# Forty dense V tiles, seven V rows to a group and batches of eight tokens

## The reference, cut to what matters

```python
def peer_ffn(hn, w_pq, sub_keys, u_tab, v_tab):      # 256 tokens, 8 heads, 16 experts a head
    ...
    expert = ia * PEER_N_KEYS + ib                   # ia, ib in 0..127
    gate = jax.nn.softmax(best_s, axis=-1)
    ...
        a = jnp.einsum('td,ted->te', xb, u_tab[eb])  # 128 U rows of 2048 for each token
        hidden = gb.astype(xb.dtype) * jax.nn.gelu(a)
        return jnp.einsum('te,ted->td', hidden, v_tab[eb])   # and 128 V rows
...
h = h + peer_ffn(rmsnorm(h, norm_ffn), ...)
return rmsnorm(h, norm_final)
```

## Time and profile before

| | us |
|---|---|
| median of 3 runs (lowest, highest) | 3092.3 (3092.18, 3098.1) |
| the profiled execution | 3086.04 |
| its span | 3084.2 |
| busy in the span: PE / DVE / ACT / POOL | 2708.9 / 2113.3 / 1146.6 / 976.6 |
| the groups of U rows, from the end of group 0 to the end of group 15 | 868.3 (1876.3 to 2744.6) |
| from there to the first dense product | 81.6 (2744.6 to 2826.2) |
| first to last dense product | 232.2 (2826.2 to 3058.4) |

### The profile page before, as it was taken

How to read it: one execution, slowest core, us unless ns; L and a number is a source line. 1 busy time by engine, 2 the same in 40 slices (tenths; PEclk the granted TensorE clock), 3 DMA queues, 4 the chain that set the end, 5 groups by cost and what they waited for, 6 DMA issues and landing times.

```text
span 3084.2 us, 34635 instructions
## 1 busy us (share of the span) xinstructions
PE 2708.9 (88%) x12198; PEld 1963.7 (64%) x12198; DVE 2113.3 (69%) x2870; ACT 1146.6 (37%) x1980; POOL 976.6 (32%) x566
## 2 busy tenths in 40 slices
PE   8999999999999999999999984666667776679997
PEld 8888788888887888999779881222223332235433
DVE  5687665555564555545555679787888888779877
ACT  5455555555553335445665540000002330034000
POOL 0011000000000000000000027777778877778854
PEclk9999999999999999999999996889898989988999
DMA  6444455555555555543344469999999999999997
GB/s 266 156 155 164 174 178 184 188 190 190 190 178 190 186 184 180 180 178 137 123 178 177 164 240 385 419 415 413 409 417 411 418 412 402 404 399 380 412 410 301
DMA packets 123586, 827.89 MB, mean 268 GB/s; under 512 B 22167, under 2 KB 22183, under 8 KB 23855
## 3 DMA queue, kind: packets, MB, share of 16 engines
q0 software_dynamic: 79392, 510.36, 40.8%
q1 hardware_dynamic: 43920, 313.73, 28.3%
q10 hardware_dynamic: 144, 2.10, 0.2%
HBM read 892.00 MB, written 4.22 MB: 291 GB/s over the span
## 4 chain that ended last, share of the span: by engine, by line
PE 61%; POOL 11%; DMA 11%; DVE 10%; issue 4%; ACT 3%; DVEq 0%; SPq 0%; ACTq 0%
PE ps L608 50%; POOL rows L1310 11%; DMA rows<-peer_u,arena 6%; PE ps L1217 4%; DVE arena L2412 3%; DMA rows<-peer_v 2%; PE ps L1228 2%; DMA rows<-peer_v,arena 1%; PE ps L713 1%; ACT arena L1771 1%; DVE arena L209 1%; DVE arena L202 0%; DVE WL L506 0%; PE ps L908 0%; PE ps L1208 0%
## 5 line engine op out<-in xcount | busy, mean ns | idle before, releaser
L506 DVE SCALAR_TENSOR_TENSOR WL<-ring,PA,WH 128x512 fp32r<-128x512 f32 x896 | 633.4, 753 | 471.0 <-ACT WH L490 454.4
L1228 PE MATMUL ps<-rows,rstd 128*128 128x512 f32 x1164 | 624.4, 689 | 303.9 <-DMA rows<-peer_v,arena 216.8
L2412 DVE CUSTOM_DVE_ANT_0 arena<-rows,arena 128x2048 f32<-128x2048 f32 x256 | 586.9, 2293 | 142.0 <-DMA rows<-peer_u,arena 113.3
L1228 PEld LDWEIGHTS ps<-rows,rstd 128*128 128x128 f32 x1164 | 244.2, 219 | 671.1 <-issue 373.1
L1310 POOL DMA_INDIRECT rows<-peer_v,arena x256 | 473.6, 1850 | 203.8 <-DVE arena L2412 82.6
L489 ACT ACTIVATE WH<-ring,PA 128x512 fp32r<-128x512 f32 x448 | 324.1, 724 | 545.1 <-PE ps L608 398.3
L1310 POOL DMA_INDIRECT rows<-peer_u,arena x256 | 450.9, 1762 | 163.4 <-DVE WL L506 79.8
L608 PE MATMUL ps<-WH,HH 128*128 128x512 f32 x1120 | 442.5, 395 | 4.3 <-DVE WL L506 4.3
L608 PE MATMUL ps<-WH,HL 128*128 128x512 f32 x1120 | 437.6, 391 | 0.0
L608 PE MATMUL ps<-WL,HH 128*128 128x512 f32 x1120 | 437.5, 391 | 0.0
L608 PE MATMUL ps<-HH,WH 128*128 128x256 f32 x1088 | 310.5, 285 | 13.3 <-DVE WL L506 13.3
(11 more groups left out here) (364 smaller groups left out, 3528.5 us busy)
## 6 DMA issues: line engine op xcount, KB each, us to landing
ring<-stream SPq DMA_DIRECT2D x292, 1024.0 KB, 4.8
rows<-peer_v POOLq DMA_DIRECT2D x32, 1024.0 KB, 14.8
rows<-peer_u,arena POOLq DMA_INDIRECT x256, 14.3
rows<-peer_v,arena POOLq DMA_INDIRECT x256, 14.4
arena<-xT SPq DMA_DIRECT2D x4, 512.0 KB, 8.9
bias_rows<-bias_scratch POOLq DMA_DIRECT2D x1, 2048.0 KB, 10.8
arena<-xT ACTq DMA_DIRECT2D x1, 2048.0 KB, 10.1
arena<-memT POOLq DMA_DIRECT2D x1, 2048.0 KB, 9.3
```

The lines of the kernel that those rows point to most:

```text
L506: ins = nc.vector.scalar_tensor_tensor(out=half_tile(WL, u)[:, s], in0=raw_half(u)[:, s], scalar=gain[d], in1=half_tile(WH, u).bitcast(f32 ...
L1228: last = mm(ps[:, 4 * tt + q, :], DIAG[:, k % DIAGS, :], rows[:, SLOTS[n % ROWS], q * CH:(q + 1) * CH], start=n == mine[0], stop=n == ends[q])
L2412: ins = V.tensor_tensor_reduce(out=JUNK, in0=rows[:, SLOTS[n % ROWS], :], in1=HN[:, tt, :], scale=1.0, scalar=0.0, op0=ALU.mult, op1=ALU.a ...
```

## The change

`N_DENSE` goes from 32 to 40, `LEAD` from 9 to 7 and `BATCH` from 16 to 8, which makes 16 batches for a tile of tokens instead of 8, at every fourth U row of groups 9 to 12 and at every second V row of the last part. Fewer lead rows leave more V rows for the last part: 151 instead of 121. Of those that belong to tile 0 (m below 23) DVE now takes every one, so that the sum of tile 0 that PE holds at ROW_LAST is that of the 105 lead rows. The larger matrices need space: IA_GATE and GROW move, the load of GROW now waits for all batches, the last norm writes its result over XN, and the squares of the last norm are written to PSUM.

```diff
-N_DENSE = 32
-LEAD = 9
-BATCH = 16
+N_DENSE = 40
+LEAD = 7
+BATCH = 8
...
     if m < DENSE_FROM:
-        return m % 5 == 4
+        return m % 5 == 4 and N_LEAD + m >= P
...
-    BATCH_AT[ROW_AT["u", 9 + _b // 2, 3 + 8 * (_b % 2)]] = (0, _b)
-    BATCH_AT[ROW_AT["v", *V_ORDER[N_LEAD + 4 * _b + 3]]] = (1, _b)
+    BATCH_AT[ROW_AT["u", 9 + _b // 4, 3 + 4 * (_b % 4)]] = (0, _b)
+    BATCH_AT[ROW_AT["v", *V_ORDER[N_LEAD + 2 * _b + 3]]] = (1, _b)
...
-        GROW = JUNK
+        GROW, _ = take(KD * TOK + KD * P, D)
...
-        FIN = HN
...
-        IA_GATE, _ = take(KD * TOK, 2, BATCH, N_DENSE)
+        IA_GATE, _ = take(N_DENSE * P, 2, BATCH, N_DENSE)
...
-            sp.wait_ge(sem("hidden"), GROUPS)
+            sp.wait_ge(sem("dense_h_kept"), TT * BATCHES)
             sp.dma_start(GROW, bass.AP(gfin_row.tensor, 0, [[0, P], [1, D]])).then_inc(sem("gfin_in"), 16)
             sp.wait_ge(sem("final_ready"), 1)
-            sp.dma_start(out[:, 0, :], FIN[:, 0, :]).then_inc(sem("out_written"), 16)
+            sp.dma_start(out[:, 0, :], XN[:, 0, :]).then_inc(sem("out_written"), 16)
...
-                ch.mark(A(FIN[:, tt, s], XN[:, tt, s], ACT.Square, accum_out=FS[:, n:n + 1]), "final_squares")
+                ch.mark(A(ps[:, 0:4, :].rearrange("p a b -> p (a b)")[:, s], XN[:, tt, s], ACT.Square, accum_out=FS[:, n:n + 1]), "final_squares")
...
-                    V.scalar_tensor_tensor(out=FIN[:, tt, cols], in0=XN[:, tt, cols], scalar=fs, in1=GROW[:, cols],
+                    V.scalar_tensor_tensor(out=XN[:, tt, cols], in0=XN[:, tt, cols], scalar=fs, in1=GROW[:, cols],
...
-                    add_sum(0, 0, 4, done, ROW_DONE[ROW_AT["v", PEER_H - 1, PEER_K - 1]][1])
+                    add_sum(0, 0, 4, done, N_LEAD)
```

More of the change, by code:

```diff
@@ L590, in _ @@
                     sp.dma_start(ring[:, s, :], stream[bass.ds(i * RING + s, 1)].rearrange("a p n -> (a p) n")).then_inc(full[s], 16)
-            sp.wait_ge(sem("hidden"), GROUPS)
+            sp.wait_ge(sem("dense_h_kept"), TT * BATCHES)
             sp.dma_start(GROW, bass.AP(gfin_row.tensor, 0, [[0, P], [1, D]])).then_inc(sem("gfin_in"), 16)
             sp.wait_ge(sem("final_ready"), 1)
-            sp.dma_start(out[:, 0, :], FIN[:, 0, :]).then_inc(sem("out_written"), 16)
+            sp.dma_start(out[:, 0, :], XN[:, 0, :]).then_inc(sem("out_written"), 16)
             for s in range(2):
                 sp.wait_ge(sem("final_ready"), 2 + s)
-                sp.dma_start(out[:, 1, s * HALF:(s + 1) * HALF], FIN[:, 1, s * HALF:(s + 1) * HALF]).then_inc(sem("out_written"), 16)
+                sp.dma_start(out[:, 1, s * HALF:(s + 1) * HALF], XN[:, 1, s * HALF:(s + 1) * HALF]).then_inc(sem("out_written"), 16)
             sp.wait_ge(sem("out_written"), 16 * 3)
```

## The result

The changed kernel takes 3105.7 us in the median of 7 runs (3104.0 to 3109.7), the one before 3091.4 in 7 runs (3085.4 to 3098.1). The ratio is 1.0047, with a 95% interval of 1.0037 to 1.0058: 14.5 us slower, between 11 and 18. The profiled execution took 3107.9 us (span 3106.0).

A forecast was written before the change was run, and what follows sets the result against it. Transfers were taken to bind the groups and dense stretch, DVE the stretch behind ROW_LAST. Terms -69 + 14 + 61 + 2.5 = +8.5 us; 8 us on the 3092.3 median gave 3100 us, range 3084 to 3112.

The forecast's parts named there:

- the forecast's own +6 to +13: Whole kernel: the band of us slower around the summed +8.5 us, given a chance of 0.42.
- DVE binds in the groups too: Rival, chance 0.12: DVE leaves transfers dry 0.5 us more in each group; sum +16.5 us, 3109 us.
- Behind ROW_LAST: From ROW_LAST to the first dense product: DVE sets the pace, 14 us longer, range +13 to +16.
- slots pin the transfers to the same place: At the first dense product POOL can be no further than the twelfth row beyond DVE, cutting whatever the groups gave.
- V rows of DVE under 2.4 us: Sign of being wrong: in the stretch behind ROW_LAST, DVE's V rows take less than 2.4 us.
- Groups: The 15 groups up to ROW_LAST: fewer rows per group, 69 us sooner.
- bound of -64: Smallest gain given for the groups: four groups' 4.4 us DVE excess and a few tenths lost at each choose.
- DVE's need without batches: In a group without batches DVE needs 49 to 50 us of 53.3, a cover of 3 to 4 us.
- Dense stretch: First to last dense product: more dense and V rows, transfers bind, 61 us longer.
- my own upper bound: Dense stretch: 24.6 more full rows at 2.59 us each, 63.7 us longer.
- bytes win: Rival, chance 0.13: transfers stay full behind ROW_LAST, the 17 us saved come through less 2.6 for GROW; about 3078 us.
- GROW: Its 1.05 MB load moves to the first dense product, where bytes bind: +2.5 us.

The follow-up runs named there:

- a_half: Changed kernel, with DVE adding only half the columns of its V rows among the first 35 behind ROW_LAST, same transfers: 3088.3 us, ratio 0.9998.
- b_lead7: Kernel before with LEAD 7 and tile 0's V rows behind ROW_LAST all on DVE; 32 dense tiles and batches of 16 stay: 3104.6 us, ratio 1.0052.
- a_noskip: Changed kernel with no index put out of bounds, so every V row moves all its 128 tokens: 3233.9 us in two runs, ratio 1.0459.
- a_early: Changed kernel with the seven V rows of the last group placed two U rows earlier: 3105.3 us, ratio 1.0043.
- a_dense6: Changed kernel with six products instead of eight for each dense tile, same transfers: 3106.4 us, ratio 1.0048.
- a_dense32: Changed kernel with 32 dense tiles instead of 40; LEAD 7, batches of 8 and the new places stay: 3112.7 us, ratio 1.0066.
- b_place: Kernel before with the new places only: GROW moved and loaded after all batches, last norm over XN, its squares to PSUM: 3090.7 us, ratio 0.9996.
- b_even: Kernel before with always the same 32 of 128 tokens left out of every V row, spread evenly over partitions: 3074.2 us, ratio 0.9945.

## Why the prediction was right or wrong, point by point

The sign, the mechanism and the place were right, and 3105.7 lies in the range; the size was short, 14.5 us for 8.5, and above the forecast's own +6 to +13. Its value is near the rival "DVE binds in the groups too" (3109), but that was not what happened: that rival puts its loss into every group, and of the 72.6 us that the transfers allow, the groups gave 67.4 ahead of the new wait.

**Behind ROW_LAST.** The step that carried the forecast, that slots pin the transfers to the same place and what DVE loses is lost, is shown by a_half and b_lead7, and by a_noskip, where more bytes left that stretch as long as it was. The instruction of 320 columns took 0.49 us, as worked out. The term itself was +11.5 for +14, and the share 0.77 where I had said 0.80. One sign of being wrong was badly put: "V rows of DVE under 2.4 us". The mean of one is 2.35 us in both kernels; the sum used the distance from one to the next, 2.44, and that held (4.82 us for two in the changed kernel).

**Groups.** -62.7 for -69, outside the bound of -64. Two steps failed. I took DVE's need without batches from its waits as 49 to 50 us; groups that run without waits show 50.7, and with four batches 55.0 to 56.2 instead of 54.5. From the end of group 0 to that of group 15 this left -67.4 (864.4 to 797.0 us). The other 4.7 are the wait at the new add. The edit `add_sum(..., N_LEAD)` waits for the last lead row, loaded behind the last U row, where the old one waited for a row seven V rows earlier. I read this line as a mere renaming of a count; a_early leaves open whether it costs anything in the end.

**Dense stretch.** With the groups, this is the term that made the size short: +72.1 in the profiled executions, and at least +65 with the others beside them, for 61 and 2.5. The count of rows was right: 26.1 MB more (120.2 less 94.05) are 24.9 rows, and I had 24.6 and GROW. What was mis-sized is the price of a row: I priced every row by its bytes, at 2.59 us for a full one (405 GB/s). That makes 1.93 us for a V row before and 1.79 after. A full row costs 2.49 us (1.0486 MB at the 421 GB/s of a_noskip). With that for the dense rows, what is left of each dense stretch is the price of a V row: before (232.2 - 29 x 2.49)/80 = 2.00 us, b_lead7 (292.9 - 29 x 2.49)/110 = 2.01, and the changed kernel, with GROW as a 38th full row, (304.3 - 38 x 2.49)/111 = 1.89. So the rate fell to 395 GB/s for two reasons: more of the stretch was V rows, which alone made 400 of 405 (b_lead7), and each had more tokens missing. I took less than my own upper bound because PE would smooth; a_dense6 shows that PE has no part.

**Bytes.** By these prices the 17 us of the "bytes win" rival were not there. Per V row a quarter of tokens missing saved not 0.63 us of 2.49 but 0.45: in the groups, (868.3 - 234 x 2.49)/140 = 2.04 us. With this price 5.7% more tokens left out of 256 rows save 256 x 0.45 x 5.7/25.3 = 26 us, eight dense rows cost 8 x 2.49 = 20, and 6 us are left; 40 tiles against 32 measured about 6 (a_dense32), though with intervals that overlap.

**GROW.** +2.5 expected, nothing found (b_place).

**Two rules that I drew on.** The page "DMA: Bandwidth & Descriptors" of the Trainium skill, section "Why a DMA increments its semaphore by 16 and not by 1", says that a transfer has landed only when all its engines are done. I weighed it for a rival and gave that 0.12. The runs fit it, 418 GB/s with the same tokens left out in every row and 405 as the data falls, but don't show an engine that waits for another. The same page of the Trainium skill, section "Specifications", gives about 358 GB/s as the HBM limit of one core, worked out there as half of what a stack gives two cores. This kernel runs on one core and moved full rows at 421, so the trace doesn't agree with 358 as a limit.

## What to carry to other kernels

Where transfers bind and a ring of slots lies between them and an engine, time is lost in stretches in which that engine is late, and a faster stretch ahead of them can't make up for it by more than the slots hold: count for each stretch what each engine needs, and move no work to the one where another already binds. Bytes saved by leaving out parts of a gather were worth less than their share here (0.45 us for 0.63), except where the same tokens were left out in every row, spread evenly over the partitions. And an edit that turns one count of a wait into another is a new wait: look up what it waits for and when that lands.

## What the runs showed of the hardware that was not expected

The rate of gathers of 128 rows of 8 KB depends on how the tokens left out are spread. The rates are from the rows above. The other two columns are counted from the records that the traces keep of each packet of queue 0 in the dense stretch: a packet of 8192 B is one row of the V table.

| rows in the stretch | left out in a V row | GB/s | mean of an 8192 B packet | over 400 ns |
|---|---|---|---|---|
| all full (a_noskip), 421 in the groups as well | 0 | 421 | 314 ns | 0.05% |
| 80 V and 29 dense rows, same 32 tokens (b_even) | 25.0% | 418 | 315 ns | 0.3% |
| 80 V and 29 dense rows, as the data falls (before) | 25.3% | 405 | 320 ns | 1.4% |
| 110 V and 29 dense rows, as the data falls (b_lead7) | 25.3% | 400 | 321 ns | 1.8% |
| 111 V and 37 dense rows, as the data falls (changed) | 31% | 395 | 325 ns | 2.6% |

The DMA share stands at 0.99 to 1.01 in all of them, so the loss can't be seen in the share, only in the rate. The packets say why the share is blind: a few of them take up to 2.2 us where most take 0.31, and the share counts them as busy. What those over 400 ns take beyond 313 ns each makes 5.4 us of every engine's time in the dense stretch before and 11.6 in the changed one, out of the 8.8 and 18.8 us by which these stretches are longer than their bytes at 421 GB/s. What such a packet waits for is open.

A token left out isn't nothing either, but it is little: it is a packet of 4 B that takes 9 to 10 ns of one engine in every one of these traces. In the earlier trace rows the gathers look like any other, but the view of the transfers from 2826.2 to 3058.4 of the kernel before counts 4531 packets under 512 B. Eighty gathers with 16 completions and some 32 tokens left out, and 29 dense rows with 16 completions, make 4304.

```profile
DMA packets 16005, 94.05 MB, mean 405 GB/s; under 512 B 4531, under 2 KB 4531, under 8 KB 4531
```

The whole execution with full rows (a_noskip) has as many packets as the changed kernel, 124738, but fewer small ones:

```profile
DMA packets 124738, 904.26 MB, mean 280 GB/s; under 512 B 13992, under 2 KB 14008, under 8 KB 15680
```

The changed kernel has 24166 small ones and 820.96 MB. So 10174 packets of 8 KB have become small ones, where 31% of 256 x 128 tokens are 10158: each token left out is one small packet in place of one of 8192 B.
